# The context's scan and softmax attention woven into the second half of the projections, and modulation chunks given to other stages

## What is computed

```
def trunk_layer(x, cx, c, c_ctx, ..., update_ctx):
    sh1, sc1, ga1, sh2, sc2, ga2 = modulation(c, w_mod, b_mod)
    sh1c, sc1c, ga1c, sh2c, sc2c, ga2c = modulation(c_ctx[None], w_mod, b_mod)
    u = (rmsnorm(x, g_mix) * (1 + sc1) + sh1) @ w_in
    uc = (rmsnorm(cx, g_mix) * (1 + sc1c) + sh1c) @ w_in
    o_gc, s_f, s_b = gla_bidir(*gla_features(gqc, ...), s_zero, s_zero)
    o_gl, _, _ = gla_bidir(*gla_features(gq, ...), s_f, s_b)
    ...
    mix = concat([pool_mixer(p), gla_output(o_gl, gg), latent_attention(ql, k_all, v_all)]) @ w_out
    x = x + ga1 * mix
    x = x + ga2 * squared_relu_mlp(rmsnorm(x, g_mlp) * (1 + sc2) + sh2, w_up, w_down)
    if update_ctx:      # layer 0 only
        mix_c = concat([pool_mixer(pc), gla_output(o_gc, ggc), context_attention(qc_, kc_, vc_)]) @ w_out
        cx = cx + ga1c * mix_c
        cx = cx + ga2c * squared_relu_mlp(...)
```

## Time and profile before

| | |
|---|---|
| runs | 2155.07 (median), 2151.92, 2157.4 us |
| profiled execution | 2152.76 us; span of its records 2151.0 us |
| TensorE busy | 1917.4 us, 89% of the span |
| VectorE, ScalarE, GpSimd busy | 1136.5, 907.0, 318.4 us |
| granted TensorE clock | 0.931 on average |
| HBM read | 317.68 MB |

### The profile page before, as it was taken

One profiled execution on the slowest core, in us unless ns is written; L12 is line 12 of the kernel. 1 busy time (PEld: TensorE's weight loads), 2 busy tenths in 40 slices (PEclk: granted clock), 3 DMA queues, 4 the chain that ended last, 5 costly groups with the idle time before them and its releaser, 6 DMA issues.

```text
span 2151.0 us, 29103 instructions
## 1 busy us (share of the span) xinstructions
PE 1917.4 (89%) x12247; PEld 1649.1 (77%) x12247; DVE 1136.5 (53%) x1602; ACT 907.0 (42%) x1403; POOL 318.4 (15%) x359
## 2 busy tenths in 40 slices
PE   4878777899999999969799968898899999989999
PEld 2765456788888888746698958788789978768997
DVE  2545447445465555565545536754355545565554
ACT  3543324345455444533444434433244444434443
POOL 1011113221131112121211110031200005200000
PEclk9999788999999999979799979989999999989999
DMA  8445263445556566432546524410155554503554
GB/s 270 140 167 186 96 198 98 150 135 167 177 173 212 185 215 199 137 112 84 156 162 191 193 73 137 138 59 1 54 163 185 173 185 168 194 1 118 195 178 137
DMA packets 217966, 320.61 MB, mean 149 GB/s; under 512 B 8550, under 2 KB 123946, under 8 KB 217452
## 3 DMA queue, kind: packets, MB, share of 16 engines
q1 hardware_dynamic: 212628, 308.96, 44.1%
q0 software_dynamic: 1744, 6.03, 0.9%
q10 hardware_dynamic: 3464, 3.75, 0.5%
HBM read 317.68 MB, written 1.05 MB: 148 GB/s over the span
## 4 chain that ended last, share of the span: by engine, by line
PE 74%; DVE 12%; ACT 6%; DMA 3%; issue 2%; POOL 2%; SPq 0%; POOLq 0%; ACTq 0%; DVEq 0%
PE ps L69 71%; DVE WLO L86 3%; PE ps L77 3%; DVE AR L96 2%; ACT WHI L80 2%; DVE AR L86 2%; DMA RAW<-in_w_mod_dram 1%; ACT AR L80 1%; POOL SM L86 1%; DMA RAW<-in_w_up_dram 1%; ACT PMD L80 1%; POOL XR L86 1%; DVE SM L99 1%; ACT XN L80 1%; ACT XR L80 1%
## 5 line engine op out<-in xcount | busy, mean ns | idle before, releaser
L86 DVE TENSOR_TENSOR WLO<-RAW,WHI 128x1024 fp32r<-128x1024 f32 (+3 forms) x506 | 592.4, 1212 | 436.2 <-ACT WHI L80 435.8
L80 ACT ACTIVATE WHI<-RAW 128x1024 fp32r<-128x1024 f32 (+3 forms) x506 | 488.2, 1014 | 416.5 <-PE ps L69 331.2
L69 PE MATMUL ps<-TH,WHI 128*128 128x256 f32 x1664 | 481.5, 289 | 27.6 <-DVE WLO L86 17.4
L69 PE MATMUL ps<-TL,WHI 128*128 128x256 f32 x1664 | 476.5, 286 | 0.0
L69 PE MATMUL ps<-TH,WLO 128*128 128x256 f32 x1664 | 476.0, 286 | 0.0
L69 PE MATMUL ps<-WHI,ARR 128*128 128x512 f32 x1120 | 356.6, 395 | 3.0 <-DVE ARR L86 1.9
L69 PEld LDWEIGHTS ps<-TH,WHI 128*128 128x128 f32 x1664 | 325.3, 195 | 38.3 <-issue 22.5
L69 PEld LDWEIGHTS ps<-TL,WHI 128*128 128x128 f32 x1664 | 325.5, 196 | 0.3
L69 PEld LDWEIGHTS ps<-TH,WLO 128*128 128x128 f32 x1664 | 325.1, 195 | 0.0
L69 PE MATMUL ps<-WHI,TH 128*128 128x512 f32 (+3 forms) x624 | 247.8, 397 | 34.6 <-DVE WLO L86 31.1
L69 PEld LDWEIGHTS ps<-WHI,ARR 128*128 128x128 f32 x1120 | 212.4, 190 | 51.9 <-issue 6.1
(11 more groups left out here) (174 smaller groups left out, 1929.8 us busy)
## 6 DMA issues: line engine op xcount, KB each, us to landing
RAW<-in_w_mod_dram SPq DMA_DIRECT2D x48, 1024.0 KB, 5.2
RAW<-in_w_up_dram SPq DMA_DIRECT2D x48, 1024.0 KB, 5.4
RAW<-in_w_down_dram SPq DMA_DIRECT2D x48, 1024.0 KB, 5.1
RAW<-in_ffn_w_in_dram SPq DMA_DIRECT2D x44, 1024.0 KB, 5.1
RAW<-in_w_in_dram SPq DMA_DIRECT2D x20, 1024.0 KB, 5.4
RAW<-in_ffn_w_out_dram SPq DMA_DIRECT2D x20, 1024.0 KB, 5.0
RAW<-in_dil_w_in_dram SPq DMA_DIRECT2D x18, 1024.0 KB, 4.8
RAW<-in_gdn_w_in_dram SPq DMA_DIRECT2D x16, 1024.0 KB, 5.7
```

What stands on the lines that cost most here:

```text
L69: return Made(None if self.eng is None else self.eng.matmul(o, l, r, start=start, stop=stop))
L80: return Made(None if self.eng is None else self.eng.activation(o, i, f, **k))
L86: return Made(None if self.eng is None else self.eng.tensor_tensor(o, a, b, op))
```

## The change: what it does

Stage C goes away as a stage. All of the context's attention (36 parts) and all that is left of its scan (22 parts) are woven into the latent tokens' projections, with five modulation chunks (5 to 9); chunk 4 moves to stage A. `work(0, 0)` begins right behind. Its first 12 parts (output product and norm) are woven with chunks 10 and 11, the first 8 parts of the latent scan and the last pooling part. Chunks 12 to 15 stay. Stage E takes chunks 16 to 21, stage G none, and chunks 22 and 23 go into the first 12 parts of `work(1, 1)`. `dve_modend` runs after chunks 3, 5, 9 and 11 of a layer, and TensorE's gate matmuls wait for the bias of their own part. The wider bank rings of stage C are not used any more.

```
+        MODS = {3: 0, 5: 4, 9: 6, 11: 10}
...
-                if ch in (3, 11):
-                    dve_modend(l, 0 if ch == 3 else 4, ch + 1)
+                if ch in MODS:
+                    dve_modend(l, MODS[ch], ch + 1)
...
-            pe.wait_ge(dve_mod, ("gain", l, 1))
+            pe.wait_ge(dve_mod, ("bias", l, 12 if jj else 6))
...
-            weave((part(p, 8), 8), (part(ga, 4), 4))
+            weave((part(p, 8), 8), (part(ga, 4), 4), (mods(range(4, 5)), 2))
...
-            weave((p, 40 + LAG - n - 16), (part(ga, 10), 10), (part(at, 12), 12), (part(pl, 3), 3), (mods(range(4, 8)), 8))
-            yield
-            weave((pl, 1), (at, ATTENTION - 12), (mods(range(8, 12)), 8), (ga, GLA[0, 0] - 16), (part(gb, 3), 3))
-            yield
-            weave((work(0, 0), working(0)), (chain(slow(gb), slow(attention(0, 1))), 2 * (GLA[0, 1] - 3 + ATTENTION)),
+            weave((p, 40 + LAG - n - 16), (ga, GLA[0, 0] - 6), (at, ATTENTION), (part(pl, 3), 3), (mods(range(5, 10)), 10))
+            yield
+            w = work(0, 0)
+            weave((part(w, 8 + NORM_PARTS), 8 + NORM_PARTS), (mods(range(10, 12)), 4), (part(gb, 8), 8),
+                  (pl, 1))
+            weave((w, working(0) - 8 - NORM_PARTS), (chain(slow(gb), slow(attention(0, 1))), 2 * (GLA[0, 1] - 8 + ATTENTION)),
                   (mods(range(12, 16)), 8))
...
-            weave((w, working(0) - 8 - NORM_PARTS), (chain(p, slow(gla(1, 0))), 20 + LAG), (mods(range(16, 20)), 8))
+            weave((w, working(0) - 8 - NORM_PARTS), (chain(p, slow(gla(1, 0))), 20 + LAG), (mods(range(16, 22)), 12))
...
-            weave((attention(1, 1), ATTENTION), (pooling(1, 1), 2), (mods(range(20, 24)), 8), (gb, GLA[1, 1] - 8))
-            yield
-            run(work(1, 1))
+            weave((attention(1, 1), ATTENTION), (pooling(1, 1), 2), (gb, GLA[1, 1] - 8))
+            yield
+            w = work(1, 1)
+            weave((part(w, 8 + NORM_PARTS), 8 + NORM_PARTS), (mods(range(22, 24)), 4))
+            yield
+            run(w)
```

More of the change, by code:

```diff
@@ L3105, in pe_program @@
             oring.set(7)
-            next(order)
-            lring.set(3, 4, 1)
-            aring.set(0, 5, 6)
             next(order)
@@ L3169, in pool_program @@
             order = common_order(pool_project, nothing, nothing, pool_gla, nothing, pool_work, lambda sq, _: pool_next(sq))
-            advance(order, 3)
+            advance(order, 2)
             pool.wait_ge(pe_gl[0], ("out", 0, 1))
@@ L3180, in pool_program @@
             pool_row("gdn")
+            next(order)
             pool.wait_ge(pe_mod, ("turn", 23))
```

## The result

| | before | after |
|---|---|---|
| first comparison, median of 4 runs each | 2156.24 us | 2125.37 us |
| profiled execution, span of its records | 2151.0 us | 2122.1 us |
| granted clock, mean | 0.931 | 0.940 |

The ratio is 0.9858, with a 95% interval of 0.9835 to 0.9882: some 31 us faster. A second comparison beside other kernels gave 0.9895 (0.9874 to 0.9915), some 23 us. The forecast was -26 us and 2129 us, range 2107 to 2150.

A forecast was written before the change was run, and what follows sets the result against it. TensorE was taken as the bound, with 74% of the chain. Terms -34.6 + 2.9 + 2 + 8 + 5 - 9.3 gave -26 us: 2152.76 becomes 2126.8, and with the median 2.3 above, 2129 us; range 2107 to 2150.

The forecast's parts named there:

- The work of the merged stage: Stages B and C as one: 101 us of TensorE work plus 27 lost, 128 us rather than 162.6, so -34.6.
- the attention steps: Rival for the merged stage: 4.5 us lost per attention step, 54 for 12 steps; +1 in all, 2156 us; chance 0.10.
- Nearly all is covered: Rival: the merged stage loses only 14 us and stage G gives back all 11.8; about -43, 2112 us; chance 0.20.
- the rotation: End of the merged stage: rotation of the last attention queries on VectorE, little covered by dense work, 8.1 us of the loss.
- my 1 us for the fifth: Merged stage: 1 us of loss for its fifth chunk, added to stage B's 18 and the rotation's 8.1.
- The slots rival: Merged stage: weight loads wait for chunks' slots, 7.6 us exposed for each of five; +12, 2167 us; chance 0.08.
- No stretch with a clock under 0.8: Sign that the forecast is right: no clock under 0.8 between 133 us and the start of `work(0, 0)`, near 264 us.
- Stage A and the head of `work(0, 0)`: Stage A +2.9 for chunk 4; head +2: 9.9 of added work less 5.8 of w_out stall and 2 covered by norm.
- the reason given: Head of `work(0, 0)`: only chunk 9 lies between the last projection tile and w_out, so both w_out loads start early.
- Stage E: Chunks 20 and 21 added without cover: 5.9 us and 1.1 of waiting for each, +8 (5 to 12).
- Stages F, G and the head of `work(1, 1)`: Stage G -9.3 for losing four chunks and a w_out split; head +5 (2 to 9) for chunks 22 and 23.
- The clock rival: Stage G: chunks kept its clock up, so 7 us aren't saved and 9 more run at half clock; -10, 2145 us; chance 0.10.

The follow-up runs named there:

- e4: Changed kernel with chunks 5 to 9 multiplying constants already there, so their ten 1 MB tiles are not loaded; 2110.42 us, ratio 0.9812.
- e6: Changed kernel with layer 0's latent projections reordered so that the rotation of the queries lies beside dense work; 2125.53 us, ratio 0.9884.
- e7: Changed kernel with chunks 4 to 11 all in the merged stage, none in stage A or the head of `work(0, 0)`; 2145.16 us, ratio 0.9974.
- e11: Changed kernel with two more float32 matmuls of 128x512 at the beginning of `work(0, 1)`; 2124.58 us, ratio 0.9887.
- e1: Changed kernel with layer 1's chunks put back: 16 to 19 in stage E, 20 to 23 in stage G; 2121.89 us, ratio 0.9864.

## Why the prediction was right, and where it wasn't

**The work of the merged stage** was put at 101 us at full clock and its loss at 27, as "the number that decides". The stage took 130.3 us from anchor to anchor, so by the same 101 the loss is 29.3. Of the 4.1 us by which -30.5 misses -34.6, 1.8 are where the stage begins (133.0 in the forecast, 134.8 in the table), and 2.3 are the loss. The nearest row, stage B, gave the right size. Had the loss followed the attention steps it would have been 54: that rival falls with the time, with `e4` (few waits left once the loads are gone) and with the transposes' waits, 2.6 us for all twelve steps. "Nearly all is covered" falls too: its loss of 14 us is half of the measured one (its sum is -43.8, by the way, where I wrote about -43).

**What the loss is made of** was only partly right. I gave 8.1 us to the rotation. The trace has 5.8 us for VectorE at that place, and `e6` shows that an earlier rotation moves the wait into the projections and gives half a microsecond. All five chunks' loads together are 11 to 14 us by `e4`; the 18 us taken over from stage B hold those of four chunks already, so how far my 1 us for the fifth was off can't be read from this. The slots rival has its mechanism in part: `e4` shows it, but at 2.2 to 2.8 us a chunk in all, where the rival asked for 7.6 each on top of the 27. Its sign, ScalarE waiting 5 us for w_in after each chunk, didn't come: ScalarE waited 10.3 us there in four waits, the longest 4.1, and stage B had 10.5 in four. Only `e7` shows such waits, with 5.2 us for each further chunk.

**Signs.** "No stretch with a clock under 0.8" didn't hold: in windows of some 10 us the merged stage has 0.66 (145 to 155 us), 0.55 (185 to 195) and 0.52 (255 to 267.5). The mean is 0.88, and TensorE was busy for 111.1 us with what I had put at 101: some 10 of the 29.3 us are clock and not waiting. `work(0, 0)` began at 267.5 us, forecast near 264.

**Stage A and the head of `work(0, 0)`**: +2.5 and +2.1, forecast +2.9 and +2. The second is right in part by luck. I added 9.9 us of work for two chunks and the scan's start, and forgot that chunk 12 and 64 scan products were in these 12 parts before. TensorE has only 21 matmuls and 3.7 us of busy time more there (44.8 to 41.1). I also took off 7.8 us of waiting, and its idle time fell by 1.6. The two errors cancel. The first w_out tiles land early, for the reason given. The norm covered nothing more than before: its waits are 12.8 us rather than 12.2.

**Stage E** took 12.1 us more, at the end of the bounds (5 to 12), forecast +8. TensorE is busy for 8.5 us more (218.98 to 210.50); the chunks' own matmuls and turns are 5.9 of it. The other 3.6 us are idle time, where I had 2.2. So what I missed is mostly the 2.6 us of busy time beyond the chunks' own.

**Stages F, G and the head of `work(1, 1)`** gave 5.7, forecast 4.3, and the terms are off by more than the sum: G 12.6 us shorter (forecast 9.3), the head 7.4 longer (forecast 5). The clock rival doesn't hold. G has a clock of 0.82 without the chunks and had 0.83 with them, so they hadn't kept it up. What TensorE waits for before transposes there, the answer to the earlier trace rows, has grown from 13.1 to 16.0 us for VectorE:

```profile
PE ps L77 <- DVE AR L86: 16.0, 2, 11.1
PE ps L77 <- ACT AR L80: 5.8, 5, 2.4
```

**What no step had**: -3.2 us in the rest of stage D, where the change moved parts of the latent scan and so shortened a wait for GpSimd (above), and -4.2 us in the delta-rule scan, in code that didn't change and without a known cause. They make up for stages B, C and E, where the forecast was too hopeful by 8.2. The sum of -26 is nearer to the measured -31 and -23 than its terms deserve.

## What to carry to other kernels

Look for the stretch where the bounding engine has neither work nor clock, take its work at full clock, and put it beside dense work: what that gains can be estimated from a neighbouring stage that is woven already. Before adding what moves in, list what is there now, since a weave spreads its streams over more stages than their names say. Then ask what else shares the ring of weight slots: a raw tile between two others delays the load of the next and makes several loads run at once, and the engine that takes tiles apart waits for them at the head of its queue, with everything else behind it. In this kernel the price rose with their number (2.2 to 2.8 us for each of five chunks, 5.2 for each of three more), so spread such tiles thin, and don't give up taking tiles apart ahead.

Measure a stage in several traces before you explain a few microseconds of it. Here the same code gave 127 to 130 us for the merged stage.

## What the runs showed of the hardware that was not expected

- A stretch with the same instructions and nearly the same waits took 277.3 and 277.6 us in the changed kernel's two profiles (mean granted clock 0.89), 281.5 in the kernel before and 281.1 in `e11` (clock 0.87). Differences of 4 us between traces of this kernel are thus not explained by an edit until the clock rows have been compared. The Trainium skill (TensorE: Matmul & The Clock Gate, What's actually happening) states that the gate's watch over the engine's activity is free-running and isn't reset when a kernel starts. That would fit; no run here tells that mechanism from another.
- In dense work one wait of 3.1 us for a weight tile was followed by 5 us at a clock of 0.53 (`e1`), nearly all of it at the lower of the clock's two levels, half speed. In the kernel before, a wait of 1.2 us at the same place left it at 1.00.
- With three more chunks in the merged stage the DMA engines' mean share there stayed the same (0.48 with five chunks, 0.47 with eight), and yet bandwidth counted where it hurt: in 5 us of ScalarE's wait in `e7` the share was 1.05 at 395 GB/s, and a load of 1 MB that ran beside two others took 10.56 us rather than 5.3. The mean share of a stage hides this. `e1`'s windows above show the same at its wait (0.88 and 0.97).
